# Up projections of a feed-forward network: each 512-column product issued as two of 256, one half of the tokens after the other

## The chip, the cores and the metric

The kernel runs on one core of one Trainium2 chip. The metric is the device time of one execution in microseconds; the median of three runs of the kernel before is 3792.21 us (3791.65 to 3793.97).

## What is computed

Two transformer layers on 512 tokens of width 1024, each of them a feed-forward network (FFN), a token mixer and a second FFN, and behind them one more block with its own mixer and an expert layer. The change lies in the four FFNs alone. With `h` of 512 x 1024 and a hidden width of 2816:

```
def _swiglu(h, w_gate, w_up, w_down):
    return (jax.nn.silu(h @ w_gate) * (h @ w_up)) @ w_down

for l in range(DEPTH):                       # DEPTH = 2
    ...
    x = x + 0.5 * g0 * _swiglu(h, ffn_w_gate[l, 0], ffn_w_up[l, 0], ffn_w_down[l, 0])
    ...
    x = x + 0.5 * g2 * _swiglu(h, ffn_w_gate[l, 1], ffn_w_up[l, 1], ffn_w_down[l, 1])
```

## The kernel before

Activations are held transposed, with 128 channels on the partitions and the 512 tokens along the free axis. Every fp32 factor is held as a sum of two fp32r numbers, a high part and the rest: `hh` and `hl` for the activations, `whi` and `wlo` for the weights. A product of a 128 x 128 weight block with 512 tokens is then three matmuls, all in one group of PSUM (line numbers are the profile's): `whi*hh` (L284), `whi*hl` (L285), `wlo*hh` (L286). Each of them loads its own 128 x 128 weights first. The language writes one call; the engine runs a weight load and a matmul, which the profile shows as PEld and PE.

Weights come as a stream of tiles of 128 x 1024 (512 KB). A tile holds the 8 blocks (KD = 8) that make one output of 128 channels x 512 tokens, so a tile is 8 x 3 = 24 matmuls. Four engines hand a tile on, each by a semaphore:

- SP loads it into `wraw` (`Stream.load`, L263), two buffers, once POOL has finished with the buffer;
- ACT rounds it into `whi` (`round`, L273), four buffers, once PE has finished the tile four back;
- POOL subtracts to get `wlo` (`rest`, L277);
- PE waits for `w_lo`, runs the 24 matmuls, and raises `w_mm` at the last.

An FFN (`ffn`) has 44 tiles of up projection, gate and up by turns, and 24 of down projection. The outputs of the up projection go to four banks `f_ps[:, 0..3]` of 512 fp32 columns: bank 0 a gate, bank 1 its up, bank 2 the next gate, bank 3 its up. ACT takes silu of a gate bank (L525), DVE multiplies it with the up bank and splits the product in two (L578, L580, L582), and PE may write a pair of banks anew when `f_prod` says that DVE has read it. The first four tiles are issued by themselves, two of them by `pair` and two by `times`. The other 40 run in a loop of 10 passes on PE, with four tiles in a pass:

```
with pe.Fori(1, KF // 2) as i:
    for j in range(4):
        pe.wait_ge(M["f_prod"], i * 2 + j // 2 + 1)
        W.times(pe, i, j, ps[:, j], hh, hl)
```

A pass is thus 96 matmuls with 96 weight loads. The order of the work is fixed by hand: each engine has its own program and waits only where a semaphore is named. Beside the FFN's own work DVE makes dot products for the modulation of later stages (L148), from rows that SP loads between the weight tiles.

Of the kernel before, what the change touches and what calls it, by code (L numbers as in the profile page):

```python
# [23 lines left out]
P = 128  # L24
D = 1024
S = 512
L = 2
KD = D // P
# [213 lines left out]
class Stream:  # L242
# [55 lines left out]
    def times(self, pe, i, j, out, xh, xl):  # L298

        self.slices(pe, i, j, out, [xh[:, k] for k in range(KD)], [xl[:, k] for k in range(KD)], 0, KD, True, True, None)  # L300

    def pair(self, pe, out, xh, xl, x_split, n=0, done=0, order=range(KD)):

        pe.wait_ge(self.M["w_lo"], n + 4)
        for at, k in enumerate(order):
            pe.wait_ge(x_split, done + at + 1)
            for j in range(2):
                mm = self.products(n + j, k, out[:, j], xh[:, k], xl[:, k], at == 0, at == KD - 1)
                if at == KD - 1:
                    mm.then_inc(self.M["w_mm"], 1)  # L310


def keep_busy(nc, T, pe, out, n, width=S):

    for _ in range(n):
        nc.tensor.matmul(out[:, 0:width], T.const[:, C_IDENT:C_IDENT + P], T.const[:, 0:width], start=True, stop=True,
                         skip_group_check=True)
# [105 lines left out]
def ffn(nc, T, layer, which):  # L423
# [13 lines left out]
    with ExitStack() as ctx:  # L437
# [16 lines left out]
        with ExitStack() as c2:  # L454
            hh = c2.enter_context(nc.sbuf_tensor("f_hh" + T.tag + str(which), [P, KD, S], F32R))
            hl = c2.enter_context(nc.sbuf_tensor("f_hl" + T.tag + str(which), [P, KD, S], F32R))
        wrow = sb("m_wrow", [P, 3, 2, D])
        prod = sb("m_prod", [P, D])
        ps = ctx.enter_context(nc.psum_tensor("f_ps" + T.tag + str(which), [P, 4, S], F32))
        psD = ctx.enter_context(nc.psum_tensor("f_psD" + T.tag + str(which), [P, 2, S], F32))  # L460
        W = Stream(nc, T, M, layer * LAYER_T + (FFN_T + PROJ_T + OUT_T if which else 0))
        Q = Sums(nc, T, M, a32[:, 0], sg, T.psN)
        norm = (nc, T, M, sg, hh, hl, gain, shift)
        with nc.Block() as block:
# [79 lines left out]
            @block.tensor  # L544
            def _(pe):
                W.ahead(pe=pe)
                keep_busy(nc, T, pe, ps[:, 3], 2)
                W.pair(pe, ps, hh, hl, M["n_lo"])
                for j in (2, 3):
                    W.times(pe, 0, j, ps[:, j], hh, hl)  # L550
                with pe.Fori(1, KF // 2) as i:
                    for j in range(4):

                        pe.wait_ge(M["f_prod"], i * 2 + j // 2 + 1)
                        W.times(pe, i, j, ps[:, j], hh, hl)
                for o in range(KD):
                    if o >= 2:
                        pe.wait_ge(M["f_res"], o - 1)
                    for c, (k0, kt) in enumerate(PIECES):
                        n = UP + 3 * o + c  # L560
                        hi = [ah[:, k] if k < KL else ahe[:, k - KL] for k in range(KF)]
                        lo = [al[:, k] if k < KL else ale[:, k - KL] for k in range(KF)]
                        W.slices(pe, n // 4, n % 4, psD[:, o % 2], hi, lo, k0, kt, c == 0, c == 2,
                                 M["f_act"] if o == 0 else None)
                Q.total(pe, psD[:, 0])
                keep_busy(nc, T, pe, psD[:, 0], 6, P)
                Q.spread(pe)
# [1977 lines left out]
```

## Time and profile before

| | |
|---|---|
| median of three runs | 3792.21 us |
| the profiled execution, its own time | 3794.71 us |
| span of its instructions | 3792.9 us |
| PE (matmuls) busy | 3469.7 us, 91%, 13968 matmuls |
| PEld (weight loads) busy | 2354.6 us, 62%, 13968 loads |
| DVE, ACT, POOL busy | 55%, 35%, 44% |
| matmuls of the up projections (`f_ps`, L284 to L286) | 3 x 1408 = 4224 |
| mean granted TensorE clock | 0.967 of full speed |

The span holds all of the execution but 1.8 us. Ends of matmuls are modelled in this profile and the bars of neighbours overlap, so the pace of PE is read from the distance of their starts.

### The profile page before, as it was taken

What the parts mean: (1) busy time and instruction counts of PE and PEld (TensorE: products, weight loads), DVE (VectorE), ACT (ScalarE), POOL (GpSimd) and SP (SyncE); (2) the same over time, 40 slices, a digit from 0 to 9 for tenths busy, and PEclk for the clock granted to TensorE, in tenths of its full rate; (3) what the DMA queues carried; (4) which work ended last, traced back from release to release, by engine and by line L of the source; (5) the groups of instructions that cost most, each with busy time, mean ns of one, the idle gap of its engine ahead of it and who ended that gap; (6) DMA issues with size and microseconds to landing.
All of it is one profiled execution on the core that took longest, in us unless ns stands there. A gap on an engine that the chain in (4) does not pass through costs nothing. (4 is left out here: it accounts for less than half of the span.)

```text
span 3792.9 us, 41813 instructions
## 1 busy us (share of the span) xinstructions
PE 3469.7 (91%) x13968; PEld 2354.6 (62%) x13968; DVE 2073.7 (55%) x3994; ACT 1312.5 (35%) x2691; POOL 1653.4 (44%) x1085
## 2 busy tenths in 40 slices
PE   8999999999999999999999999997777777777777
PEld 6888776788888887676888876663333333333333
DVE  5635357433335454475332065577777767666664
ACT  3332226433233323155333233433233233233222
POOL 2446432444544455224444533344444444444442
PEclk9999999999999999999999999998899999999899
DMA  6536320133435354201223321479999999999997
GB/s 242 185 116 245 133 100 1 51 101 98 169 135 194 135 212 176 99 18 35 89 94 100 106 79 56 158 265 421 421 421 422 421 421 421 422 421 421 422 421 312
DMA packets 140418, 830.71 MB, mean 219 GB/s; under 512 B 15712, under 2 KB 16352, under 8 KB 63840
## 3 DMA queue, kind: packets, MB, share of 16 engines
q0 software_dynamic: 73728, 536.90, 34.3%
q1 hardware_dynamic: 66528, 291.77, 21.8%
q8 instruction: 86, 1.41, 0.2%
q14 instruction: 76, 0.62, 0.0%
HBM read 826.52 MB, written 2.10 MB: 218 GB/s over the span
## 5 line engine op out<-in xcount | busy, mean ns | idle before, releaser
L277 POOL TENSOR_TENSOR wlo<-wraw,whi 128x1024 fp32r<-128x1024 f32 x357 | 902.6, 2533 | 1179.0 <-ACT whi L273 1178.7
L273 ACT ACTIVATE whi<-wraw 128x1024 fp32r<-128x1024 f32 x357 | 377.5, 1058 | 664.0 <-DMA wraw<-in_wts 353.4
L284 PE MATMUL f_ps<-f_hh,whi 128*128 128x512 f32 x1408 | 549.5, 390 | 1.6 <-DVE f_hl L405 1.6
L286 PE MATMUL f_ps<-f_hh,wlo 128*128 128x512 f32 x1408 | 547.9, 389 | 0.0
L285 PE MATMUL f_ps<-f_hl,whi 128*128 128x512 f32 x1408 | 547.9, 389 | 0.0
L2083 PE MATMUL g_psF<-g_low,g_diagb 128*128 128x512 f32 x660 | 328.1, 649 | 95.5 <-ACT g_diagb L2149 95.0
L578 DVE TENSOR_TENSOR f_a<-f_sg,f_ps 128x512 f32<-128x512 f32 x88 | 60.5, 687 | 511.2 <-PE f_ps L286 496.6
L2083 PE MATMUL g_psF<-g_own,g_diagb 128*128 128x512 f32 x576 | 279.9, 636 | 65.2 <-ACT g_diagb L2149 64.8
L2083 PE MATMUL g_psF<-g_top,g_diagb 128*128 128x512 f32 x524 | 261.0, 649 | 74.3 <-ACT g_diagb L2149 74.3
L2137 ACT ACTIVATE g_dotb<-g_dotb 128x4 f32<-128x4 f32 (+2 forms) x146 | 29.9, 205 | 861.9 <-DVE g_dotb L2238 861.9
L2083 PEld LDWEIGHTS g_psF<-g_low,g_diagb 128*128 128x128 f32 x660 | 134.6, 209 | 285.3 <-issue 285.1
L284 PEld LDWEIGHTS f_ps<-f_hh,whi 128*128 128x128 f32 x1408 | 264.3, 188 | 63.6 <-DVE f_hl L405 5.1
L286 PEld LDWEIGHTS f_ps<-f_hh,wlo 128*128 128x128 f32 x1408 | 264.3, 188 | 55.4
L285 PEld LDWEIGHTS f_ps<-f_hl,whi 128*128 128x128 f32 x1408 | 264.3, 188 | 53.8
L2016 POOL DMA_INDIRECT g_low<-in_uv,idx x165 | 188.4, 1142 | 221.2 <-PE g_psF L2083 180.8
L2238 DVE CUSTOM_DVE_ANT_0 g_low<-g_low,xtok 128x1024 f32<-128x1024 f32 x165 | 199.2, 1225 | 120.1 <-DMA g_low<-in_uv,idx 116.5
L2083 PEld LDWEIGHTS g_psF<-g_own,g_diagb 128*128 128x128 f32 x576 | 115.6, 205 | 223.8 <-issue 223.8
L2016 POOL DMA_INDIRECT g_own<-in_uv,idx x144 | 157.4, 1093 | 199.1 <-PE g_psF L2083 168.0
L2083 PEld LDWEIGHTS g_psF<-g_top,g_diagb 128*128 128x128 f32 x524 | 105.9, 207 | 222.7 <-issue 222.7
L2238 DVE CUSTOM_DVE_ANT_0 g_own<-g_own,xtok 128x1024 f32<-128x1024 f32 x144 | 176.6, 1243 | 103.7 <-DMA g_own<-in_uv,idx 95.5
L2016 POOL DMA_INDIRECT g_top<-in_uv,idx x131 | 150.3, 1147 | 184.0 <-PE g_psF L2083 154.0
L2238 DVE CUSTOM_DVE_ANT_0 g_top<-g_top,xtok 128x1024 f32<-128x1024 f32 x131 | 158.7, 1225 | 102.4 <-DMA g_top<-in_uv,idx 99.2
(416 smaller groups left out, 6470.3 us busy)
## 6 DMA issues: line engine op xcount, KB each, us to landing
wraw<-in_wts SPq DMA_DIRECT2D x359, 512.0 KB, 3.5
m_wrow<-in_ada SPq DMA_DIRECT2D x44, 1024.0 KB, 6.9
m_erow<-in_ada SPq DMA_DIRECT2D x28, 1024.0 KB, 5.3
p_wt<-in_wtok SPq DMA_DIRECT2D x2, 3168.0 KB, 10.0
p_wt<-in_w SPq DMA_DIRECT2D x2, 3072.0 KB, 9.6
g_low<-in_uv,idx POOLq DMA_INDIRECT x165
g_own<-in_uv,idx POOLq DMA_INDIRECT x144
g_top<-in_uv,idx POOLq DMA_INDIRECT x131
```

The costliest lines, as they stand in the source:

```text
L273: self.nc.scalar.activation(self.T.whi[:, j % 4], self.T.wraw[:, j % 2], ACT.Copy).then_inc(self.M["w_hi"], 1)
L277: self.nc.gpsimd.tensor_tensor(self.T.wlo[:, j % 4], self.T.wraw[:, j % 2], self.T.whi[:, j % 4].bitcast(F32), ALU.subtract).then_inc(self ...
L284: self.nc.tensor.matmul(out, hi, xh, start=first, stop=False)
L285: self.nc.tensor.matmul(out, hi, xl, start=False, stop=False)
L286: return self.nc.tensor.matmul(out, lo, xh, start=False, stop=last)
L578: nc.vector.tensor_tensor(a32[:, g], sg[:, g], ps[:, 2 * g + 1], ALU.mult).then_inc(M["f_prod"], 1)
L2016: nc.gpsimd.indirect_dma_start(slots[slot_of[j]], None, T.d["uv"], bass.IndirectOffsetOnAxis(ap=T.idx[:, j // TOP, j % TOP:j % TOP + 1], a ...
L2083: mm = nc.tensor.matmul(psF[:, t % 2, c], diag[:, s % 4, k], slots[slot_of[j]][:, D + c * S:D + (c + 1) * S], start=False, stop=j % (PH * ...
L2137: nc.scalar.activation(dot[:, s % 4, 0:size], dot[:, s % 4, 0:size], ACT.Gelu_apprx_tanh).then_inc(M["g_gelu"], 1)
L2238: nc.vector.tensor_tensor_reduce(u, u, xtok[:, j // (PH * TOP)], 1.0, 0.0, ALU.mult, ALU.add, dot[:, s % 4, k:k + 1]).then_inc(M["g_dot"], 1)
```

## The change

The four tiles of a loop pass are issued by a new function, `by_halves`, in place of `times`. It goes over the tile twice: all 24 products for the tokens 0 to 255, with matmuls of 256 columns into the first half of the bank, then the same 24 for the tokens 256 to 511. Each of the 48 matmuls loads its weights. The waits are the same, one for `w_lo` ahead of the first matmul and one for `f_prod` ahead of the tile, and `w_mm` is raised once, at the last matmul of the second half. The first four tiles of each FFN, the down projections and all other products stay as they were.

```diff
+    def by_halves(self, pe, i, j, out, xh, xl):
+
+        pe.wait_ge(self.M["w_lo"], i * 4 + j + 3)
+        for a in range(2):
+            t = slice(a * S // 2, (a + 1) * S // 2)
+            for k in range(KD):
+                w = slice(k * P, (k + 1) * P)
+                hi, lo = self.T.whi[:, j % 4, w], self.T.wlo[:, j % 4, w]
+                self.nc.tensor.matmul(out[:, t], hi, xh[:, k, t], start=k == 0, stop=False, skip_group_check=True)
+                self.nc.tensor.matmul(out[:, t], hi, xl[:, k, t], start=False, stop=False, skip_group_check=True)
+                mm = self.nc.tensor.matmul(out[:, t], lo, xh[:, k, t], start=False, stop=k == KD - 1,
+                                           skip_group_check=True)
+        mm.then_inc(self.M["w_mm"], 1)
...
                     for j in range(4):
 
                         pe.wait_ge(M["f_prod"], i * 2 + j // 2 + 1)
-                        W.times(pe, i, j, ps[:, j], hh, hl)
+                        W.by_halves(pe, i, j, ps[:, j], hh, hl)
```

PE's program at the head of the loop, before. The names are the destination and, behind the arrow, tokens and weights:

```order
L551 UNCONDITIONAL_BRANCH
L551 ISA
L290 ISA [waits ffn0_f_prod]
L284 MATMUL f_ps<-f_hh,whi 128x512 [waits ffn0_w_lo]
L285 MATMUL f_ps<-f_hl,whi 128x512
L286 MATMUL f_ps<-f_hh,wlo 128x512
```

The same place in the changed kernel, whose lines stand 14 further down:

```order
L565 UNCONDITIONAL_BRANCH
L565 ISA
L304 ISA [waits ffn0_f_prod]
L310 MATMUL f_ps<-f_hh,whi 128x256 [waits ffn0_w_lo]
L311 MATMUL f_ps<-f_hl,whi 128x256
L312 MATMUL f_ps<-f_hh,wlo 128x256
```

Before, 24 such rows follow a wait for `w_lo` and then comes the next tile. Now 48 rows of half the width follow it. Nothing else is moved on PE, and the programs of the other engines are the same.

## Rows read from the trace of the kernel before

**Rows 1.** The page: busy time of each engine, share, instructions
```profile
PE 3469.7 (91%) x13968; PEld 2354.6 (62%) x13968; DVE 2073.7 (55%) x3994; ACT 1312.5 (35%) x2691; POOL 1653.4 (44%) x1085
```
**Rows 2.** The page: costliest groups; busy, mean ns, idle before, releaser
```profile
L277 POOL TENSOR_TENSOR wlo<-wraw,whi 128x1024 fp32r<-128x1024 f32 x357 | 902.6, 2533 | 1179.0 <-ACT whi L273 1178.7
L284 PE MATMUL f_ps<-f_hh,whi 128*128 128x512 f32 x1408 | 549.5, 390 | 1.6 <-DVE f_hl L405 1.6
L286 PE MATMUL f_ps<-f_hh,wlo 128*128 128x512 f32 x1408 | 547.9, 389 | 0.0
L285 PE MATMUL f_ps<-f_hl,whi 128*128 128x512 f32 x1408 | 547.9, 389 | 0.0
L578 DVE TENSOR_TENSOR f_a<-f_sg,f_ps 128x512 f32<-128x512 f32 x88 | 60.5, 687 | 511.2 <-PE f_ps L286 496.6
```
**Rows 3.** Timeline of PE, end of an up projection: start, duration, engine, line
```profile
287.47 0.39 PE L286 MATMUL f_ps<-f_hh,wlo 128*128 128x512 f32 x1
...
288.83 0.39 PE L286 MATMUL f_ps<-f_hh,wlo 128*128 128x512 f32 x1
289.06 0.39 PE L284 MATMUL f_psD<-f_ah,whi 128*128 128x512 f32 x1
```
**Rows 4.** Busy time by stretch, `f_ps` alone: PE, PEld, DVE, ACT, PEclk, DMA
```profile
80.00:280.00 200.00, 200.00 (x885) 165.58 (x884) 13.06 (x19) 10.72 (x18) 1.00 0.44 155
89.30:92.90 3.60, 3.60 (x17) 2.98 (x17) 0.00 (x0) 0.00 (x0) 1.00 0.53 159
```
**Rows 5.** Timeline: fp32 (not fp32r) matmuls of 256 columns
```profile
2241.76 3.61 PE L1574 MATMUL m_psZ<-m_wt,xT 128*128 128x256 f32 x16
```
**Rows 6.** Timeline: matmuls of 64 columns behind full weight loads
```profile
612.08 0.97 PEld L1104 LDWEIGHTS psN<-kcmp,z 128*128 128x128 f32 x8
612.19 1.00 PE L1104 MATMUL psN<-kcmp,z 128*128 128x64 f32 x8
```
**Rows 7.** Timeline of PE in a stretch with the clock at half
```profile
2344.87 0.63 PE L286 MATMUL m_psZ<-m_xh,wlo 128*128 128x512 f32 x1
2345.30 0.63 PE L284 MATMUL m_psZ<-m_xh,whi 128*128 128x512 f32 x1
2345.72 0.63 PE L285 MATMUL m_psZ<-m_xl,whi 128*128 128x512 f32 x1
2346.15 0.63 PE L286 MATMUL m_psZ<-m_xh,wlo 128*128 128x512 f32 x1
```
**Rows 8.** Timeline: a weight load that comes late, with the matmul before it
```profile
1126.47 0.39 PE L286 MATMUL f_ps<-f_hh,wlo 128*128 128x512 f32 x1
1126.67 0.19 PEld L284 LDWEIGHTS f_ps<-f_hh,whi 128*128 128x128 f32 x1 [0.23 <-DVE f_hl L405]
1126.70 0.47 PE L284 MATMUL f_ps<-f_hh,whi 128*128 128x512 f32 x1
```
**Rows 9.** Timeline of PE: the first fp32r matmuls behind a pause
```profile
2190.22 0.39 PE L285 MATMUL m_psZ<-m_xl,whi 128*128 128x512 f32 x1
2190.45 0.40 PE L286 MATMUL m_psZ<-m_xh,wlo 128*128 128x512 f32 x1
2190.69 0.39 PE L284 MATMUL m_psZ<-m_xh,whi 128*128 128x512 f32 x1
2190.92 0.40 PE L285 MATMUL m_psZ<-m_xl,whi 128*128 128x512 f32 x1
```
**Rows 10.** Busy time by stretch, attention of layer 0, all engines
```profile
642.30:653.90 11.60, 11.18 (x132) 9.04 (x130) 8.43 (x25) 7.18 (x26) 6.05 (x11) 1.00 0.01 3
```
**Rows 11.** DMA queues, 70 to 280 us: packets, MB, share of 16 engines
```profile
q1 hardware_dynamic: 7387, 33.21, 44.6%
q14 instruction: 1, 0.01, 0.0%
```
**Rows 12.** The page, DMA queue of PE's instructions, whole span
```profile
q8 instruction: 86, 1.41, 0.2%
```
**Rows 13.** One line's instructions: the loop's branch (ns min/median/max, first and last start)
```profile
L551 PEldq COMPARE_BRANCH  x40: 76/208/235, 89.3 to 2058.6; - x40
```
**Rows 14.** One line's instructions: weight loads of `f_ps` (ns min/median/max)
```profile
L284 PEld LDWEIGHTS f_ps<-f_hh,whi x1408: 186/188/188, 49.1 to 2061.6; 128*128 128x128 f32 x176
```

## The prediction

> **What bounds the kernel now.** I read the page's first part, then its groups, then the timeline and the stretches of the place that the change touches. PE has matmuls in flight for 91% of the span and no other engine is above 62% [rows 1]. That share is a mean over stages; what counts is the up projection. There the three matmul groups of `f_ps` show next to no idle time ahead of them (1.6 us in 4224 matmuls, all at the start of the FFNs), while POOL stands idle 1179.0 us waiting for ACT and DVE 496.6 us waiting for these very matmuls [rows 2]. In the stretch from 80 to 280 us, inside one loop, PE's bars cover 200.00 of 200.00 us at the full clock of 2.4 GHz (granted 1.00) [rows 4]. So the loop is bound by PE's own pace, and a nanosecond more for each matmul is a nanosecond more in the result.
>
> The pace: six starts lie between 287.47 and 288.83 us, so one matmul takes 1.36/6 = 0.2267 us, and the next one, which belongs to the down projection, follows at the same distance [rows 3]. 200/0.2267 is 882, which fits the 885 bars that touch the stretch [rows 4]. Streaming 512 columns at one a cycle of 2.4 GHz is 512/2.4 = 213.3 ns. There are **13.4 ns more** for each matmul, and the whole question is what they hang on: on the matmul, or on its columns.
>
> **The change, part by part.**
>
> *Matmuls.* 4 FFNs x 10 passes x 4 tiles x 24 = 3840 matmuls of 512 columns become 7680 of 256. The columns are the same in sum. So are the waits, the data and the semaphores. What is added is 3840 matmuls' worth of whatever a matmul costs beside its columns, and 3840 weight loads.
>
> What can that be? No row shows an fp32r matmul of 256 columns, so I bound it. Three rows narrow it down.
> (a) The 13.4 ns are no collision with the next weight load. Where that load comes 0.20 us after the matmul's start, it overlaps only its last 0.03 us, and the next matmul is still let in after 1126.70 - 1126.47 = 0.23 us [rows 8].
> (b) They are not array cycles that are always paid. With the clock at half, 1.2 GHz, the same matmuls start 0.427 us apart (three intervals in 1.28 us) [rows 7], which is 512/1.2 = 426.7 with nothing on top. Something beside the array, which keeps its own speed, is hidden there and shows at the full clock.
> (c) Plain fp32 matmuls go over their data more slowly: 256 columns in (3.61 - 0.38)/15 = 0.2154 us, which is two cycles a column (213.3) and about 2 ns [rows 5]. (Their bar of 0.38 is taken off for the last one.) They ask for half the data per cycle, and the extra is nearly gone.
> So fp32r at full clock is limited where operands are fetched. A fetch can be slow by a gap between two matmuls (fixed: 13.4 each) or by its rate (17/16 of the time for every column). From below, the rate reading gives 0 for a second matmul. From above, take the longest distance behind a pause, 0.24 us [rows 9], whose excess over 213.3 is some 27 ns; as these are rounded starts and the four give 0.233 on average, 20 ns is the fair upper value. I take **13.4 ns**: an operand stream that is set up anew for each instruction and cannot be overlapped with the one before is the simplest thing that both vanishes at half clock and at half the data rate, and 13.4 is what the nearest rows, the same instruction with the same operands, show in steady state. A rate of exactly 16/17 has no cause that I can point to in a row, for the pace is the same whatever DVE, ACT and the DMAs do beside it (up and down stage show one pace) [rows 3, 4].
> A matmul of 256 then takes 106.7 + 13.4 = 120 ns, a pair of them 240 instead of 226.7: 3840 x 13.4 = **+51 us**.
>
> *Weight loads.* A load's bar is 188 ns [rows 14], longer than the 120 ns, but loads are pipelined: eight in a row take 0.97 us, so (0.97 - 0.19)/7 = 0.111 us from one to the next, with matmuls of only 64 columns behind them [rows 6]. Loads of the same shape in the new loop would need 111 ns against 120: hidden, with 9 ns to spare. Cost nothing; the cover is the matmul itself. If a matmul of 256 took less than 111, the load would be the pace. The upper bound of this term is that the whole bar must pass before the next load: (2 x 188 - 226.7) x 3840 = +573 us. The pipelined loads speak against it [rows 6].
>
> *Issue.* The sequencer must now hand over a pair of load and matmul every 120 ns. In the attention it keeps up 132 matmuls and 130 loads in 11.6 us, 88 ns a pair [rows 10]. The loop's branch takes 208 ns [rows 13], and it runs ahead of the work: the first is at 89.3 us, while its pass, the 192nd matmul from 49 us on, ends at 93.0, 16 pairs later (17 bars touch that stretch) [rows 4, 13]. With 16 pairs of 120 ns, the queue still covers 1.9 us, nine times the branch. Nothing.
>
> *Other engines.* They get more time: a tile lasts 24 x 0.240 = 5.76 us instead of 5.44, against 2.53 us of POOL [rows 2]. The raised `w_mm` comes 0.32 us later per tile, and nobody behind it was the bound. What is late next: the down projection starts 12.8 us later in each FFN, with all of its inputs ready no earlier than before relative to PE. It runs at PE's pace too [rows 3] and so gives nothing back.
>
> *Sum.* Against the profiled execution's own 3794.71 us: +51 gives 3846. The median of the runs is 2.5 us lower, so 3792.2 + 51 = **3843 us**, 1.4% slower.
>
> The Trainium skill, "TensorE: Matmul & The Clock Gate", section "Back-to-back issue gap", gives N/2.4 + 2.5 ns for a matmul of N columns, with the cost per matmul at 2.5 ns. By it the sum would be 3840 x 2.5 = +10 us, an estimate of 3802. The fp32 rows agree with it (215.4 ns for 512 cycles) and the fp32r rows don't (226.7 against 215.8), so the row decides, and the rule's result stands among the rivals, worked out from rows.
>
> **The rivals.**
>
> *Rate, not gap.* The excess belongs to the columns. Then two halves cost what the whole did, 3792, or, if of the 13.4 ns the 2 that every plain fp32 matmul shows [rows 5] are fixed and 11.4 go with the columns, 3840 x 2 = +8: 3800. For it: the pace is the same everywhere. Against it: nothing that would cause it. The page's formula named above belongs here.
>
> *An unsettled stream.* Behind a pause the first matmuls lie 0.23 to 0.24 us apart and settle at 0.2267 only later [rows 9]. With 9 ns between load and matmul the new loop may never settle. An excess of 17 to 20 ns a matmul gives 2 x (106.7 + 17) - 226.7 = +20.7 to +26.7 ns a pair: +79 to +102, 3871 to 3895. Against it: at 111 ns with 64 columns [rows 6] load and matmul run in lockstep without trouble.
>
> *Faster.* The operand stream falls behind only in long matmuls, where a store in front of the array has run dry. A half of 256 columns would then be over before, and the pace would fall to what the weight loads allow, 0.111 us [rows 6]: 3840 x (2 x 0.111 - 0.2267) = -18 us, 3774. It decides where the excess per matmul falls below 6.6 ns. Against it: in a row of matmuls without a pause such a store has no time to fill.
>
> *The loop outgrows the instruction store.* In straight code PE fetches its instructions in blocks: 86 of 1.41 MB/86 = 16 KB [rows 12]. In the loop none is fetched between 70 and 280 us; the one packet is of another queue [rows 11]. So a body of 96 pairs stays inside. One of 192 pairs may not. A fetch takes about 0.002 x 16 x 3792.9/86 = 1.4 us [rows 12]; two in a row at each of 36 returns to the loop's head, less the 1.9 us that the queue covers, are 36 x (2.8 + 0.2 - 1.9) = +40 on top of the 51: 3883.
> The Trainium skill, "Runtime: NRT & Kernel Launch", section "Instruction fetch mechanics", says that a taken branch to a target outside a window of two pages of 16 KiB has to fetch it first, and in the same section gives PE a store of 128 KiB. No run here shows which of the two holds. By the first, a body of 192 pairs would be a page and a half and might lie across three.
>
> *Weights in full.* The load's whole bar is paid, +573 us: 4365. Against it: the loads at 111 ns [rows 6].
>
> *The change doing less than it says* is excluded by the program's own order: 48 matmuls of 256 columns stand behind each wait.
>
> **How the numbers follow.** Gap of 13.4 (forecast): 0.55. Rate: 0.15, of which 0.09 lie within 0.2% and 0.06 above it. Unsettled: 0.14. Faster: 0.05. Instruction store: 0.07. Weights in full: 0.04. The predicted time is that of the likeliest, 3843. The range of 3796 to 3895 leaves out the faster case, the full load and about half of the rate case (its lower end, 3792), 0.14 together, and the far end of the unsettled stream and the instruction store, some 0.03. About 0.2% of this kernel, 7.6 us, is what a measurement can tell from no change. Faster by more: 0.05. Within it: 0.09. Slower: 0.86.
>
> **What would show it.** In the changed trace, starts of the new matmuls in the loop 120 ns apart (113 for the rate, 111 for the faster case, 124 and more for an unsettled stream, 188 for full loads); a pass of 192 matmuls lasting 23.0 us instead of 21.8, the loop of the first FFN ending near 302 us; no idle time of PE ahead of `f_ps`; down projections at 0.2267 as before; no packet of q8 inside the loop, and no hole in PE at the 36 returns. Wrong would be a pace within 2 ns of 113, or more than 127, or holes at the branch.

## The result and the profile after

The changed kernel takes **3846.94 us** (median of four runs, 3843.58 to 3849.18); the kernel before, measured beside it, 3791.93 us (3791.25 to 3793.97). The ratio is 1.0140, with an interval of 1.0128 to 1.0152: 1.4% slower, 55 us. The forecast was 3843, with 51 us more. The two profiled executions, 3794.71 and 3846.12 us, lie 51.4 us apart, and their spans 51.5.

The profile page of the changed kernel, its busy engines and its costliest groups, beside [rows 1, 2]:

```profile
span 3844.4 us, 49493 instructions
...
PE 3525.2 (92%) x17808; PEld 2556.3 (66%) x17808; DVE 2085.9 (54%) x3994; ACT 1312.1 (34%) x2691; POOL 1657.2 (43%) x1085
...
L277 POOL TENSOR_TENSOR wlo<-wraw,whi 128x1024 fp32r<-128x1024 f32 x357 | 907.2, 2545 | 1224.5 <-ACT whi L273 1224.1
L312 PE MATMUL f_ps<-f_hh,wlo 128*128 128x256 f32 x2560 | 724.5, 283 | 0.0
...
L310 PE MATMUL f_ps<-f_hh,whi 128*128 128x256 f32 x2560 | 724.5, 283 | 0.0
...
L310 PEld LDWEIGHTS f_ps<-f_hh,whi 128*128 128x128 f32 x2560 | 491.5, 192 | 0.2
...
L592 DVE TENSOR_TENSOR f_a<-f_sg,f_ps 128x512 f32<-128x512 f32 x88 | 60.5, 688 | 549.7 <-PE f_ps L312 520.4
```

There are 3840 more matmuls and as many more loads. No new wait is there: ahead of the new matmuls (L310 to L312) PE is idle for 0.0 us, and the others only wait longer for PE. POOL's idle time behind ACT went from 1178.7 to 1224.1 us, DVE's behind `f_ps` from 496.6 to 520.4. The mean of 283 ns is a modelled bar, longer than the distance to the next matmul, and says nothing about the pace.

The pace stands in the timeline of PE inside the loop, one matmul to a row (start, duration):

```profile
149.80 0.28 PE L310 MATMUL f_ps<-f_hh,whi 128*128 128x256 f32 x1
149.92 0.28 PE L311 MATMUL f_ps<-f_hl,whi 128*128 128x256 f32 x1
...
151.00 0.28 PE L311 MATMUL f_ps<-f_hl,whi 128*128 128x256 f32 x1
```

Ten distances in 1.20 us: **0.120 us** where 0.2267 stood [rows 3]. By the exact starts in the trace, 7665 of the 7676 distances of the loop are 120 ns. Busy time by stretch for `f_ps`, beside [rows 4], has 1669 bars in 200 us and so says the same, 200/0.120 = 1667:

```profile
80.00:280.00 200.00, 200.00 (x1669) 200.00 (x1668) 12.38 (x18) 10.16 (x17) 1.00 0.41 149
```

The weight loads follow at the same distance and are never the ones that are late:

```profile
150.04 0.19 PEld L310 LDWEIGHTS f_ps<-f_hh,whi 128*128 128x128 f32 x1
150.16 0.19 PEld L311 LDWEIGHTS f_ps<-f_hl,whi 128*128 128x128 f32 x1
```

Where the loop of the first FFN ends, the old pace is back after five matmuls (by the starts 234, 235, 229, 232 and 231 ns from 300.28 us on, and then 227):

```profile
300.16 0.28 PE L312 MATMUL f_ps<-f_hh,wlo 128*128 128x256 f32 x1
300.28 0.40 PE L284 MATMUL f_psD<-f_ah,whi 128*128 128x512 f32 x1
300.51 0.40 PE L285 MATMUL f_psD<-f_al,whi 128*128 128x512 f32 x1
...
302.12 0.39 PE L286 MATMUL f_psD<-f_ah,wlo 128*128 128x512 f32 x1
302.35 0.39 PE L284 MATMUL f_psD<-f_ah,whi 128*128 128x512 f32 x1
```

The branch of the loop, and the DMA queues from 90 to 290 us, beside [rows 13, 11]. PE's instructions (q8) have no row in the second view:

```profile
L565 PEldq COMPARE_BRANCH  x40: 76/207/235, 90.9 to 2110.8; - x40
```
```profile
q1 hardware_dynamic: 6507, 28.93, 40.2%
```

**Where the time went.** Worked out from the starts of the first and the last matmul into `f_ps` of each FFN, in us. The first is the first of four fillers from a constant tile (`keep_busy`), which run 2.4 us ahead of the first product:

| part | before | after | difference |
|---|---|---|---|
| four up projections | 242.08, 242.09, 242.07, 242.07 | 255.00, 254.95, 254.98, 254.98 | +51.6 |
| between them | 458.08, 126.71, 462.45 | 459.64, 127.03, 461.02 | +0.5 |
| behind the last | 1730.6 | 1731.6 | +1.0 |

Added matmuls times the fixed cost, 960 x 13.3 ns = 12.8 us, against 12.9 us measured in each stage. The other 1.5 us are more than made up by the start, which is 1.6 us earlier (first product at 47.56 against 49.16 us). The medians differ by 55 us rather than 51, and no trace shows the 4 us more: in the profiled runs below with all halves the up projections keep to 255.0 within 0.1 us, while the rest of the span moves by up to 4 us (2820.4 to 2824.5 us).

### The profile page after: what moved, and what is told of

The parts are those of the page before. It is cut to its first block and busy times, and to the rows that moved or that the text cites. A ratio compares the mean times of both kernels' runs of the same rounds, so it can differ in the third digit from the quotient of the medians.

```text
span 3844.4 us, 49493 instructions
## 1 busy us (share of the span) xinstructions
PE 3525.2 (92%) x17808; PEld 2556.3 (66%) x17808; DVE 2085.9 (54%) x3994; ACT 1312.1 (34%) x2691; POOL 1657.2 (43%) x1085
## 5 line engine op out<-in xcount | busy, mean ns | idle before, releaser
L277 POOL TENSOR_TENSOR wlo<-wraw,whi 128x1024 fp32r<-128x1024 f32 x357 | 907.2, 2545 | 1224.5 <-ACT whi L273 1224.1
L312 PE MATMUL f_ps<-f_hh,wlo 128*128 128x256 f32 x2560 | 724.5, 283 | 0.0
L311 PE MATMUL f_ps<-f_hl,whi 128*128 128x256 f32 x2560 | 724.5, 283 | 0.0
L310 PE MATMUL f_ps<-f_hh,whi 128*128 128x256 f32 x2560 | 724.5, 283 | 0.0
L310 PEld LDWEIGHTS f_ps<-f_hh,whi 128*128 128x128 f32 x2560 | 491.5, 192 | 0.2
L311 PEld LDWEIGHTS f_ps<-f_hl,whi 128*128 128x128 f32 x2560 | 491.5, 192 | 0.2
L312 PEld LDWEIGHTS f_ps<-f_hh,wlo 128*128 128x128 f32 x2560 | 491.5, 192 | 0.0
L592 DVE TENSOR_TENSOR f_a<-f_sg,f_ps 128x512 f32<-128x512 f32 x88 | 60.5, 688 | 549.7 <-PE f_ps L312 520.4
```

What stands on the lines that cost most here:

```text
L277: self.nc.gpsimd.tensor_tensor(self.T.wlo[:, j % 4], self.T.wraw[:, j % 2], self.T.whi[:, j % 4].bitcast(F32), ALU.subtract).then_inc(self ...
L310: self.nc.tensor.matmul(out[:, t], hi, xh[:, k, t], start=k == 0, stop=False, skip_group_check=True)
L311: self.nc.tensor.matmul(out[:, t], hi, xl[:, k, t], start=False, stop=False, skip_group_check=True)
L312: mm = self.nc.tensor.matmul(out[:, t], lo, xh[:, k, t], start=False, stop=k == KD - 1, skip_group_check=True)
L592: nc.vector.tensor_tensor(a32[:, g], sg[:, g], ps[:, 2 * g + 1], ALU.mult).then_inc(M["f_prod"], 1)
```

## The experiments

Every kernel is the changed one with one edit, where nothing else is said. "Stage" is the time from the first to the last matmul into `f_ps` of an FFN, fillers included, 242.1 us before and 255.0 after the change. "By the starts" means by the exact starts in the trace. The kernel before took 3794.29 us beside the first four (median of seven), 3797.17 beside the next four (seven), 3790.20 beside three more (one run) and 3793.38 beside the last (fifteen).

### Half the dose

```diff
-                        W.by_halves(pe, i, j, ps[:, j], hh, hl)
+                        (W.times if j % 2 else W.by_halves)(pe, i, j, ps[:, j], hh, hl)
```

> Only the gate tiles (every second tile of the loop) are issued by halves: 1920 added matmuls instead of 3840. Theory, a fixed gap of 13.4 ns for each fp32r matmul: +25.7 us, about 3818; starts 120 ns apart in the gate tiles and 226.7 in the up tiles. Rival, a cost that comes with the longer loop body and not with the count (instruction fetch, branch): a body of 144 pairs is still longer than 128, so most of the 51 us would stay, about 3840. Rival, unsettled stream: changing between two widths every tile gives distances of 230 to 237 behind each change, about 3820 to 3830.

Measured: 3823.30 us (3818.04 to 3824.95), ratio 1.0072, interval 1.0055 to 1.0088. Only the gate tiles are halved, and half of the loss comes: stages of 248.9 us, +6.8 where 480 x 13.3 ns = 6.4 is the count's share. The last 0.4 us come with the changes of width. Behind each change to the full width come 233, 236, 228, 233 and 230 ns before 227 is back, 0.55 us a stage; behind each change to the half width the first distance is 113 ns instead of 120, which gives 0.15 back. The cost goes by the number of matmuls. It is not one price for a longer body or for a new loop.

### Both halves side by side

```diff
+            for c, (u, x) in enumerate(((hi, xh), (hi, xl), (lo, xh))):
+                for a in range(2):
+                    t = slice(a * S // 2, (a + 1) * S // 2)
+                    mm = self.nc.tensor.matmul(out[:, t], u, x[:, k, t], start=k == 0 and c == 0, ...
```

The same weights are now loaded twice in a row, and both halves of the bank are open at once. In this form the first 256 tokens most likely lose their first product, `whi*hh` of block 0 (see the last section); the work is the same.

> Each product's two halves stand next to each other, so the second half reloads the very weights that the first has just used. Same count, 7680 matmuls of 256. Theory (gap per matmul): 120 ns as in the changed kernel, 3843 to 3847. Rival, the extra is a price of the weight load or of taking new weights: reloading the same ones could be cheaper, below 120 ns and towards 113, 3792 to 3820. Rival, writing to alternate halves of one bank costs something: above 120 ns.

Measured: 3845.72 us (3843.65 to 3850.39), ratio 1.0137, interval 1.0120 to 1.0153. Distances of 120 ns in 7668 of 7676, stages of 254.95 to 255.01 us. The timeline of PE, which puts two matmuls in a row of the view (distance of rows 0.24 us):

```profile
149.91 0.40 PE L311 MATMUL f_ps<-f_hh,whi 128*128 128x256 f32 x2
150.16 0.40 PE L311 MATMUL f_ps<-f_hl,whi 128*128 128x256 f32 x2
150.40 0.40 PE L311 MATMUL f_ps<-f_hh,wlo 128*128 128x256 f32 x2
```

For the time it doesn't matter whether the weights are others or the same, nor in which order the halves come.

### The loop written out

```diff
-                with pe.Fori(1, KF // 2) as i:
+                for i in range(1, KF // 2):
```

> PE's loop of 10 passes is written out, with halves as in the changed kernel; PE then fetches 960 x 4 pairs in straight code, one block of 16 KB each 128 pairs, 15.4 us. Theory (neither the branch nor the fetch costs anything): the same time as the changed kernel within 0.1%, 3843 to 3849, and 120 ns. Rival, a few us of the 55 belong to the returns of the loop: lower by up to 4 us. Rival, fetching at this pace stalls PE: higher, with holes at the block borders.

Measured: 3840.85 us (3839.54 to 3848.85), ratio 1.0127, interval 1.0110 to 1.0144. PE now has no branch, and fetches all of its instructions, as the page's DMA part shows:

```profile
q8 instruction: 143, 2.34, 0.2%
```

Stages of 254.97 to 254.98 us: neither the branch nor the fetch is a part of the 12.9. The 54 packets more than in the changed kernel stand for 4 x 9 x 192 x 2 = 13,824 instructions, so one takes 54 x 16,384/13,824 = 64 bytes. A body of 192 pairs is then 24.6 KB, one and a half blocks.

### A body of 960 pairs

```diff
+                with pe.Fori(0, 2) as n:
+                    for u in range(5):
+                        for j in range(4):
...
+                            W.by_halves(pe, n * 5 + (u + 1), j, ps[:, j], hh, hl)
```

> Two passes of five old passes each on PE: a body of 960 pairs, 1920 instructions, 7.5 blocks of 16 KB. Theory 1, the store holds 8 blocks (128 KB): no block fetched in the second pass, or a single one, and the same time, 3843 to 3849. Theory 2, the store holds only a few blocks: the one return of each FFN fetches its target, then block by block anew, 7 or 8 more packets per FFN (30 in all, against 89 plus those of the longer code), and a hole of 1 to 3 us of PE minus the 1.9 us that the queue covers, at most +5 us over four FFNs.

Measured: 3861.32 us (3858.35 to 3863.72), ratio 1.0178, interval 1.0161 to 1.0195; stages of 262.4, 256.7, 259.9 and 256.7 us. Here the return to the head does cost. The branch (minimum, median, maximum in ns), the timeline of PE behind it, and the DMA queues from 185 to 300 us:

```profile
L565 PEldq COMPARE_BRANCH  x8: 79/1706/5162, 182.8 to 2124.7; - x8
```
```profile
184.71 0.28 PE L312 MATMUL f_ps<-f_hh,wlo 128*128 128x256 f32 x1
186.41 0.38 PE L310 MATMUL f_ps<-f_hh,whi 128*128 128x256 f32 x1 [1.42 <-DVE f_a L593]
...
187.58 0.28 PE L310 MATMUL f_ps<-f_hh,whi 128*128 128x256 f32 x1
190.69 0.58 PE L311 MATMUL f_ps<-f_hl,whi 128*128 128x256 f32 x1 [2.83 <-issue]
...
191.29 0.41 PE L310 MATMUL f_ps<-f_hh,whi 128*128 128x256 f32 x1
191.50 0.41 PE L311 MATMUL f_ps<-f_hl,whi 128*128 128x256 f32 x1
191.71 0.41 PE L312 MATMUL f_ps<-f_hh,wlo 128*128 128x256 f32 x1
191.93 0.41 PE L310 MATMUL f_ps<-f_hh,whi 128*128 128x256 f32 x1
```
```profile
q8 instruction: 9, 0.15, 0.5%
```

The four branches back took 3.3, 3.4, 5.2 and 3.3 us, more than the queue of waiting pairs covers, and the whole second pass was fetched anew. The first hole's row names `f_a`, but that product reads the other pair of banks; what came late was the branch, which ran from 182.8 to 186.1 us. This is what the rival of the instruction store looks like when it comes true, and nothing of it stands in the changed kernel. Behind the second hole of the first FFN the clock is at its lower level for 6.8 us, in the third FFN for 3.4 us behind a hole of 3.24 us, and in the other two, with one hole of 1.4 to 1.5 us each, not at all. At the lower level the matmuls of 256 columns lie 0.213 us apart, which is 256/1.2: as in [rows 7], nothing on top at half clock.

### A body of 384 pairs

```diff
+                with pe.Fori(0, 5) as n:
+                    for u in range(2):
...
+                            W.by_halves(pe, n * 2 + (u + 1), j, ps[:, j], hh, hl)
```

> Five passes of two old passes each on PE, by halves: a body of 384 pairs, 768 instructions, three blocks of 16 KB. Theory 1 (the store holds the three blocks or more behind the sequencer): no packet of q8 inside the loop after its first pass, no hole, 254.98 us for each up projection. Theory 2 (it holds the two blocks that the changed kernel's body of 1.5 needs, plus the next): 4 returns per FFN with a refetch, a hole of 1.7 to 3.5 us each as in the one return of the body of 7.5 blocks, 7 to 14 us more per up projection, and some 12 more packets per FFN.

Measured: 3842.31 us (one run), stages of 254.96 us, 120 ns throughout, the branch at its old price, and no packet of q8 between 98 and 297 us:

```profile
L565 PEldq COMPARE_BRANCH  x20: 76/208/226, 112.0 to 2107.0; - x20
```

### A body of 768 pairs

```diff
+                for i in (1, 2):
...
+                with pe.Fori(0, 2) as n:
+                    for u in range(4):
...
+                            W.by_halves(pe, n * 4 + (u + 3), j, ps[:, j], hh, hl)
```

Two old passes are written out, two passes of four follow.

> By halves, two old passes written out and then two passes of four on PE: a body of 768 pairs, 1536 instructions, six blocks of 16 KB. A body of three blocks ran without a refetch, one of 7.5 lost 1.7 to 7.5 us in each up projection and fetched it all again. Theory 1 (a store of eight blocks of which one is being filled and one may be cut by the body's place): fits, 254.98 us an up projection, no packet of q8 after the first pass. Theory 2 (four blocks): refetch, 1.7 to 7.5 us more per up projection, and six more packets per FFN.

Measured: 3854.72 us (one run). Only the first FFN fetched anew (its branch took 4557 ns, its stage 261.9 us), the other three ran at 254.95 to 254.98 with branches of 213 to 239 ns. The branch, and the queues from 185 to 300 us:

```profile
L570 PEldq COMPARE_BRANCH  x8: 76/146/4557, 206.0 to 2119.9; - x8
```
```profile
q8 instruction: 10, 0.16, 0.6%
```

By 64 bytes an instruction 768 pairs fill six blocks, and with the waits between them touch seven or, as the body happens to lie, eight (an estimate). Six blocks stayed in three FFNs of four, seven and a half in none, three and one and a half in all.

### Quarters

```diff
-            t = slice(a * S // 2, (a + 1) * S // 2)
+        for a, b in ((0, 128), (128, 256), (256, 384), (384, 512)):
+            t = slice(a, b)
```

> Each product of the loop as four of 128 columns, one quarter of the tokens after the other. Theory (gap of 13.4 ns and loads that follow each other at 111 ns at best): streaming and gap are 53.3 + 13.4 = 67 ns, so the weight load is the pace, 111 ns; 4 x 111 - 226.7 = +217 ns a product, +835 us, about 4628. Rival A, the 120 ns of the halves was itself the pace of an fp32r weight load and no gap of the stream: 120 ns again, 4 x 120 - 226.7 = +253 ns, +973 us, about 4766. Rival B, loads don't bound: 67 ns, 4 x 67 - 226.7 = +40 ns, +154 us, about 3947.

Measured: 4639.42 us (one run); stages of 453.3 us. By gap alone a matmul of 128 would take 53.3 + 13.3 = 67 ns. The timeline of PE has 16 distances in 1.78 us, 0.111:

```profile
149.73 0.28 PE L310 MATMUL f_ps<-f_hh,whi 128*128 128x128 f32 x1
...
151.51 0.28 PE L311 MATMUL f_ps<-f_hl,whi 128*128 128x128 f32 x1
```

Here the weight loads are the pace, at the 0.111 us of [rows 6] (mean 111.65 ns by the starts): the distance is the same for matmuls of 64 and of 128 columns, and the issue of pairs has gone at 88 ns [rows 10]. The 9 ns that separated the change from this floor were real.

### Wide and narrow

```diff
+        for a, b in ((0, 384), (384, 512)):
+            t = slice(a, b)
```

> Each product of the loop as one of 384 columns (tokens 0 to 383) and one of 128. Theory (fixed gap): the wide ones 160 + 13.4 = 173.4 ns apart, the narrow ones at the load's 111 ns; together +57.7 ns a product, +222 us, about 4014. Rival (the extra time is set by the load or comes in steps of 120 ns): anything but 173 for the wide ones, 180 if the excess were the sixteenth part of a longer fetch, 170 if it went with the columns.

Measured: 4016.36 us (one run); stages of 298.67 us. The wide matmuls, ten distances in 1.74 us:

```profile
153.15 0.33 PE L310 MATMUL f_ps<-f_hh,whi 128*128 128x384 f32 x1
...
154.89 0.33 PE L311 MATMUL f_ps<-f_hl,whi 128*128 128x384 f32 x1
```

By the starts they are 173 and 174 ns once settled, and 384/2.4 = 160. So the fixed part is 13.3 at 256, 384 and 512 columns alike, and a share that goes with the columns isn't there. The narrow ones stand at the load's floor, 110 to 114 ns, but for the first distance in each tile, 60 ns. That is 6.7 ns over its 53.3, as the 113 of the half dose is 6.3 over 106.7: the 13.3 belong to the settled stream, and the first matmul behind a change to a narrower one pays about half.

### Two of three products read as bf16

The kernel before, with the second and third product of every streamed block read as bf16: the upper two bytes of each fp32r number, by a step of two. The values lose their lower bits.

```diff
+        top = lambda v: v.bitcast(BF16)[:, 1::2]
+        self.nc.tensor.matmul(out, top(hi), top(xl), start=False, stop=False)
+        return self.nc.tensor.matmul(out, top(lo), top(xh), start=False, stop=last)
```

> The kernel before, with the second and third product of every streamed weight block (rounded weights x rest of the activations, rest of the weights x rounded activations) read as bf16: the upper halves of the same fp32r words, by a step of two, 512 columns as before. These two products are small corrections and lose some of their last bits. Theory (the gap shows only where the operand fetch is the limit, as in fp32r at the full clock): half the data, the gap falls from 13.4 to the 2 ns of plain fp32, 215.5 ns apart instead of 226.7, 5632 matmuls x 11 ns = -62 us, about 3731. Rival A, the gap belongs to the swap of weights or to issue, whatever the type: 226.7 stays, 3792. Rival B, words of two bytes at a step of four are fetched like fp32r: 226.7 stays too, and only a dense bf16 operand could tell.

Measured: 3849.62 us (3848.39 to 3852.70), ratio 1.0144, interval 1.0127 to 1.0161; stages of 249.6 us. The expectation was missed, and by its sign. The timelines of PE and of PEld:

```profile
120.18 0.40 PE L286 MATMUL f_ps<-f_hl,whi 128*128 128x512 bf16 x1
120.42 0.39 PE L287 MATMUL f_ps<-f_hh,wlo 128*128 128x512 bf16 x1
120.44 0.60 PE L284 MATMUL f_ps<-f_hh,whi 128*128 128x512 f32 x1
120.88 0.40 PE L286 MATMUL f_ps<-f_hl,whi 128*128 128x512 bf16 x1
```
```profile
120.42 0.19 PEld L284 LDWEIGHTS f_ps<-f_hh,whi 128*128 128x128 f32 x1
120.88 0.10 PEld L286 LDWEIGHTS f_ps<-f_hl,whi 128*128 128x128 bf16 x1 [0.27 <-issue]
```

From bf16 to bf16 it takes 0.24 us, and three products take 0.70 us instead of 0.68. The load of bf16 weights behind an fp32r matmul comes only as that matmul ends (120.88, where the next one starts too). The load of fp32r weights behind a bf16 matmul runs under it, as usual (120.42). This kernel mixes two things, a change of type twice in three and the step of two. The next two take them apart.

### Type by runs, with the step

Each tile of the loop as 16 fp32r matmuls, then its eight `wlo*hh` as bf16 by a step of two, in the tile's own bank.

```diff
+            mm = self.nc.tensor.matmul(out, lo.bitcast(BF16)[:, 1::2], xh[:, k].bitcast(BF16)[:, 1::2], start=False,
+                                       stop=k == KD - 1)
```

> The same order, but the eight bf16 matmuls of a tile read the upper halves of the fp32r words, at a step of two, and go to their own bank. Theory A (the words at a step of two are fetched as slowly as whole fp32r words, and more): 240 ns between them as in the run before, 1280 x 13.4 = +17 us and 4 for the changes of type: about 3815. Theory B (the 240 belonged to the change of type in each block): 227 or 215.5, 3783 to 3798.

Measured: 3798.26 us (one run); stages of 243.65 us. By the starts, the distances between the bf16 matmuls are 240 ns for the first in a tile (120 are on record) and then 225 (880 of 1040 on record; the other 40 span a matmul whose record is missing).

### Type by runs, dense

The same order, but the eight bf16 matmuls read dense rows and write to a bank that nobody reads, so `wlo*hh` is left out of the loop's tiles.

```diff
+            mm = self.nc.tensor.matmul(self.spare, lo.bitcast(BF16)[:, 0:P], xh[:, k].bitcast(BF16)[:, 0:S], start=True,
+                                       stop=True, skip_group_check=True)
```

> Products of 512 columns as before, but in the loop's tiles the 16 fp32r ones come first and the eight of wlo x hh are replaced by bf16 matmuls over neighbouring words of two bytes, written to a bank that nobody reads: this part of the result is left out. They only measure a pace. Theory (the gap is the fetch of fp32r, 2048 bytes a partition and matmul, too slow to be overlapped): half the bytes, about 215.5 ns between bf16 matmuls, 227 between the fp32r ones; 1280 x -11 = -14 us, and a change of type twice a tile, which cost some 24 ns a block of three in the run before, +4 us: about 3783. Rival (the gap belongs to every matmul that reads one column a cycle, whatever its bytes): 226.7, about 3796. The mixed run before had 240 ns from one bf16 matmul to the next; if dense ones show that too, bytes have nothing to do with it.

Measured: 3782.14 us (one run). The timeline of PE:

```profile
122.69 1.90 PE L313 MATMUL f_psD<-f_hh,wlo 128*128 128x512 bf16 x8
124.24 0.58 PE L308 MATMUL f_ps<-f_hh,whi 128*128 128x512 f32 x1
124.66 0.39 PE L309 MATMUL f_ps<-f_hl,whi 128*128 128x512 f32 x1
```

By the starts, the first of the seven distances from bf16 to bf16 is 227 ns and the other six are 215 or 216 (mean 215.8). Where the operand stream needs half the bytes, 2.5 of the 13.3 ns are left, much as with plain fp32 [rows 5], which takes two cycles a column. By the step of two, in the run above, 225.0 - 213.3 = 11.7 ns are left, nearly all. The first fp32r matmuls behind the change are late: the last bf16 and the first fp32r together take 446 ns instead of 443, and then come 224, 231, 236, 228, 232, 231 before 227 is back, some 26 ns. The change to bf16 costs some 14 (230 and 227 where 227 and 216 would stand). A tile thus takes 5393 ns instead of 24 x 226.7 = 5440: of 8 x 10.9 = 87 ns some 40 are lost.

### A version that uses it

POOL writes `wlo` of the up projection's tiles 3 to 43 as dense bf16 into a tile `wls`, and a bf16 copy `hb` of `hh` once for each FFN. PE runs 16 fp32r matmuls and then the eight with bf16, all of them in one group. `wlo*hh` is then taken with bf16 factors, nothing is left out.

```diff
+        for k in range(KD):
+            w = slice(k * P, (k + 1) * P)
+            hi = self.T.whi[:, j % 4, w]
+            self.nc.tensor.matmul(out, hi, xh[:, k], start=k == 0, stop=False)
+            self.nc.tensor.matmul(out, hi, xl[:, k], start=False, stop=False)
+        for k in range(KD):
+            w = slice(k * P, (k + 1) * P)
+            mm = self.nc.tensor.matmul(out, self.T.short[:, j % 4, w], xb[k], start=False, stop=k == KD - 1)
```

> A whole version of what the dense bf16 run measured: in the 41 tiles from the fourth on, the eight products of wlo x hh run behind the 16 fp32r ones, in the same PSUM group, from dense bf16 copies. POOL writes wlo as bf16 at once (the same subtraction), and makes the bf16 copy of hh at the head of the FFN, 8 copies of 512 columns. [...] Theory: the up stage falls from 242.08 to about 238.5 us as in the run with unread bf16 products, 4 x -3.6 = -14 us, 3778 against 3792, ratio 0.9962. Rival A: POOL's eight copies come ahead of its first weight tile and the fourth tile starts late; PE waits up to 5 us per FFN at 50 to 65 us, which would eat it: 3785 to 3795. Rival B: bf16 matmuls into the bank of the fp32r ones cost more than into a bank of their own: 240 ns and 3798 or more.

Measured: **3787.02 us** (3779.27 to 3789.56, eleven runs) against 3793.38 (3789.29 to 3798.21, fifteen) of the kernel before: ratio 0.9982, interval 0.9973 to 0.9991. It beats both kernels, by 0.18% the one before. The page, its groups:

```profile
L318 POOL TENSOR_TENSOR wls<-wraw,whi 128x1024 bf16<-128x1024 f32 x164 | 407.8, 2489 | 435.6 <-ACT whi L273 435.6
L308 PE MATMUL f_ps<-f_hh,whi 128*128 128x512 f32 x1312 | 541.9, 413 | 0.0
...
L312 PE MATMUL f_ps<-f_hb,wls 128*128 128x512 bf16 x1064 | 271.2, 381 | 4.5
```

Stages of 240.6 us, 1.5 less each, 6 us in all, where 14 were expected. The bf16 matmuls, now in the tile's own bank, keep to the 216 ns of the dense run, and a tile takes 5393 ns as there, so that 41 x 46.7 ns = 1.9 us are won in a stage from its first product on (237.8 us instead of 239.7). 0.4 us of it are lost ahead of the first product, which waits for DVE's `f_hl`. That took 1.18 us with POOL's copies running beside it (the first two rows), and 0.75 in the kernel before (the third); that the copies slow it is likely, and no run took them away.

```profile
47.44 1.18 DVE L424 SCALAR_TENSOR_TENSOR f_hl<-f_sg,mod,f_hh 128x512 fp32r<-128x512 f32 x1
47.47 1.62 POOL L529 CAST f_hb<-f_hh 128x512 bf16<-128x512 f32 x2 [46.96 <-ACT f_hh L415]
```
```profile
48.26 0.75 DVE L405 SCALAR_TENSOR_TENSOR f_hl<-f_sg,mod,f_hh 128x512 fp32r<-128x512 f32 x1
```

The 4.5 us of idle time in the row of L312 are none: 84 of the 1312 bf16 matmuls have no record (1064 and, under another name, 164 are there), each leaves 53 ns uncovered, 84 x 53 ns = 4.5 us, and the tiles take 5393 or 5394 ns with such a gap or without. The rest of what was missed was in the expectation: it rested on a stage of the dense run that left out its last eight matmuls, 1.75 us. The edit goes the right way but is worth little.

## Why the prediction was right

**The pace of the kernel.** The reading of PE as the only bound held: 51.6 us of matmuls became 51.6 us of stages and 51.5 of span, and everything else only waited longer.

**A gap of 13.4 ns for each matmul, not a share of the columns.** This was the step on which all hung, chosen between 0 and 20 ns. It is shown now by three widths:

| matmul | distance | columns at 2.4 GHz | rest |
|---|---|---|---|
| fp32r, 256 columns | 120.0 ns | 106.7 | 13.3 |
| fp32r, 384 | 173.3 | 160.0 | 13.3 |
| fp32r, 512 | 226.7 | 213.3 | 13.3 |
| bf16 dense, 512 | 215.8 | 213.3 | 2.5 |
| bf16 by a step of two, 512 | 225.0 | 213.3 | 11.7 |
| fp32r, 256, clock at 1.2 GHz | 213 | 213.3 (at 1.2) | 0 |

The reasons given for it held too, in so far as runs could reach them: the rest vanishes at half clock for the new width as for the old, and falls to 2.5 ns with half the bytes. By the 2.5 ns that the Trainium skill, "TensorE: Matmul & The Clock Gate", section "Back-to-back issue gap", adds to N/2.4 in the gap that it calls that of an isolated matmul, the change would have cost 3840 x 2.5 = 10 us, an estimate. The dense bf16 row agrees with that figure, and the fp32r rows don't. What the engine does in those 13 ns was only argued: that it is the fetch of the operands fits all of these numbers, but no run looks inside. Every matmul here has a weight load of its own, so one might put the 13.3 ns down to the load. The plain fp32 matmuls of [rows 5] speak against it: their loads are as long as those of fp32r (190 ns against 188), and only 2 ns are left over.

```profile
L1574 PEld LDWEIGHTS m_psZ<-m_wt,xT x64: 187/190/190, 2241.5 to 2282.8; 128*128 128x128 f32 x64
```

**Weight loads hidden, 9 ns to spare.** Right: 120 ns against 111. Loading the same weights twice in a row gave the same 120, and quarters ran onto the floor at 111.65. The floor was read from matmuls of 64 columns of another stage, and it carried over.

**Issue and branch, nothing.** Right: 207 ns at the branch, no hole, and written out without any branch the stages are the same.

**Other engines and the down projections.** Right: they start 12.9 us later against 12.8 forecast, run at 0.227 us from their sixth matmul on and give nothing back. The loop's end came at 300.2 us instead of 302; it began 1.6 us earlier.

**The rivals.** *Rate* (113 ns) and *faster* (111) fall with 120. *Unsettled stream* is real at a change of width or type, at 228 to 236 ns, and costs 0.4 us a stage in the half dose, but a loop of 256 columns alone settles at once. *Full loads* fall with 120 as well. The *instruction store* has its effect, with a branch of 3.3 to 5.2 us, but from six or seven blocks on rather than from one and a half. The rule of two pages of 16 KiB in the Trainium skill, "Runtime: NRT & Kernel Launch", section "Instruction fetch mechanics", would, as I read it, have had the bodies of 384 and 768 pairs fetched at every return, and the changed one where it lies across three pages; only one return, of the body of 768, was. The 128 KiB that the same section gives PE, eight such blocks, fit the bodies of up to three blocks. That seven and a half blocks never stayed they explain only if a body may not fill the store to the end, which no run shows.

The 4 us between forecast and median (51 against 55) show in no term of the sum: the profiled executions differ by 51.4, and the ranges of the two kernels' runs are 2.7 and 5.6 us wide. The halves side by side and the loop written out, at the same 120 ns, came out 51.4 and 46.6 us above the kernel beside them. That the profiled pair came within 0.5 us of the forecast is therefore in part luck; the stages, 51.6 against 51, are not.

## What to carry to other kernels

A matmul's price is its columns plus something fixed, and the fixed part must be read from the trace for the type at hand; here 13.3 ns for fp32r, so matmuls as wide as the bank allows. Two widths in one trace would have told gap from rate before any change was made; where there is but one, a stretch at half clock and a type with fewer bytes narrow it. Below (111 - 13.3) x 2.4 = 234 columns, an estimate from these rows, the weight loads take over at 111 ns. Different types are best kept in long runs, since a change to bf16 and back loses about 40 ns.

## What was not expected of the hardware

- A load of bf16 weights behind an fp32r matmul doesn't run under it: PEld stands idle for 0.27 us first, in the trace of the products read as bf16. The other way round the load runs under the matmul. Type by type in threes, bf16 loses more than it saves (0.70 against 0.68 us).
- Reading bf16 by a step of two takes 225 ns for 512 columns, 240 for the first behind fp32r; dense it is 216 and 227.
- A body of 96, 192 and 384 pairs stays in PE's instruction store, one of 768 in three FFNs of four, one of 960 in none. A branch that must fetch took 3.3 to 5.2 us, PE stood idle behind it (1.42 and 2.83 us in the first FFN of the body of 960), and behind the holes of 2.83 and 3.24 us the clock was at 1.2 GHz for 6.8 and 3.4 us. What decides which blocks are dropped stays open.
- With both halves of a bank open at once, the start flag of the second half's first matmul seems to make the first half lose what it had summed, its first product: the output of that kernel is off by a relative 0.119, while the change itself, where the second half starts only when the first is done, has nothing of it. That it is the flag was argued; no run tried it alone.
